# Moving the dilated keys to ScalarE's DMA queue, and the window copies to other places and depths, in a decoder step on one core

## The reference, cut to what matters

```python
# mixing: one projection to q, k, v of two groups of 8 heads
oa_s = stick_breaking(qa_s, k_all, v_all, pos_s, bias_l)     # k_all, v_all: 16 pages a sample
ext_k = jnp.concatenate([cache_dil_k[layer], kb_s], axis=1)  # 2048 old rows and the new one
ext_v = jnp.concatenate([cache_dil_v[layer], vb_s], axis=1)
ob_s = dilated_attention(qb_s, ext_k, ext_v, ...)            # reads 321 of the 2049 rows
dk_s.append(ext_k[:, DEC_SEQ:]); dv_s.append(ext_v[:, DEC_SEQ:])   # outputs: moved by one row
# feed-forward, for each of 256 + 8 rows: 8 heads choose 16 of 16384 experts
u = expert_u[expert]
act = jax.nn.gelu(jnp.einsum('thkd,td->thk', u, h))
return jnp.einsum('thk,thkd->td', (g * act).astype(h.dtype), expert_v[expert])
```

## Time and profile before

| | before |
|---|---|
| median of 3 runs | 1211.17 us (1208.58 to 1219.85) |
| profiled execution, device time | 1215.47 us |
| its span, first to last instruction | 1213.8 us |
| PE, DVE, ACT, POOL busy | 75%, 52%, 29%, 35% of the span |
| bytes moved by DMA | 481.21 MB, mean 396 GB/s |
| share of the DMA engines' time | 76.0% POOL's queue, 22.1% SP's |
| chain that ended last | DMA 46%, PE 30%, issue 8%, DVE 8% |

### The profile page before, as it was taken

One profiled execution on the slowest core, in us unless ns is written; L12 is line 12 of the kernel. 1 busy time (PEld: TensorE's weight loads), 2 busy tenths in 40 slices (PEclk: granted clock), 3 DMA queues, 4 the chain that ended last, 5 costly groups with the idle time before them and its releaser, 6 DMA issues.

```text
span 1213.8 us, 13371 instructions
## 1 busy us (share of the span) xinstructions
PE 909.9 (75%) x3662; PEld 423.6 (35%) x3662; DVE 635.5 (52%) x1604; ACT 351.8 (29%) x959; POOL 420.2 (35%) x430
## 2 busy tenths in 40 slices
PE   2797986668676879964778877877587777777783
PEld 0342443445232448831323322333233322323231
DVE  4200106553222544223776777777777777777755
ACT  0000001463121012221333233323433444244323
POOL 1201323112231000211455554545454455555551
PEclk9799988777898889977999999999999999999996
DMA  9999999988999899999999999999989999999996
GB/s 366 424 379 400 378 365 364 397 338 351 373 392 413 281 367 378 388 396 393 410 414 428 420 428 427 428 428 428 428 357 427 428 427 428 428 428 428 427 427 272
DMA packets 72826, 481.21 MB, mean 396 GB/s; under 512 B 9953, under 2 KB 10306, under 8 KB 27346
## 3 DMA queue, kind: packets, MB, share of 16 engines
q0 software_dynamic: 54720, 377.53, 76.0%
q1 hardware_dynamic: 18066, 103.17, 22.1%
HBM read 477.41 MB, written 70.32 MB: 451 GB/s over the span
## 4 chain that ended last, share of the span: by engine, by line
DMA 46%; PE 30%; issue 8%; DVE 8%; ACT 3%; POOL 2%; SPq 2%; POOLq 0%; DVEq 0%; ACTq 0%
DMA R<-in_uv,idst 29%; PE ps L968 11%; DMA out_dil_v_s<-in_dil_v 6%; DMA R<-in_sb_v,vrow 5%; PE ps L919 5%; PE ps L874 2%; PE ps L576 2%; POOL R L480 2%; DMA R<-in_sb_k 2%; DVE R L1770 2%; DMA vrow<-in_vrow 2%; PE ps L739 2%; PE ps L602 1%; DMA R<-in_uv,idec 1%; ACT wgt L1241 1%
## 5 line engine op out<-in xcount | busy, mean ns | idle before, releaser
L968 PE MATMUL ps<-R,diag 128*128 128x512 f32 x1024 | 491.9, 630 | 168.8 <-ACT diag L1260 167.3
L480 POOL DMA_INDIRECT R<-in_uv,idst x256 | 313.7, 1225 | 365.6 <-PE ps L968 294.6
L1770 DVE CUSTOM_DVE_ANT_0 R<-R,H 128x1024 f32<-128x1024 f32 x264 | 319.3, 1224 | 201.7 <-DMA R<-in_uv,idst 190.7
L968 PEld LDWEIGHTS ps<-R,diag 128*128 128x128 f32 x1024 | 195.7, 199 | 465.0 <-ACT diag L1260 252.0
L1238 ACT ACTIVATE gel<-dots 128x2 f32<-128x2 f32 x132 | 26.8, 203 | 403.9 <-DVE dots L1770 403.9
L576 PE MATMUL ps<-R,HT 128*128 128x512 f32 x192 | 94.3, 631 | 3.9 <-DMA R<-in_wts 3.9
L1260 ACT ACTIVATE diag<-const,wgt 128x128 f32<-128x128 f32 x256 | 88.9, 394 | 14.7 <-PE ps L968 1.4
L310 POOL DMA_INDIRECT R<-in_sb_v,vrow x32 | 30.4, 951 | 114.5 <-PE ps L739 90.2
L432 POOL DMA_DIRECT2D R<-in_wts x24 | 12.8, 541 | 157.3 <-PE ps L874 57.2
L301 POOL DMA_DIRECT2D R<-in_sb_k x64 | 34.7, 542 | 86.5 <-issue 85.9
L1241 ACT ACTIVATE wgt<-gel,gst 128x1 f32<-128x1 f32 x264 | 63.3, 287 | 4.3
(11 more groups left out here) (282 smaller groups left out, 828.6 us busy)
## 6 DMA issues: line engine op xcount, KB each, us to landing
R<-in_wts POOLq DMA_DIRECT2D x48, 1024.0 KB, 17.0
out_dil_k_s<-in_dil_k SPq DMA_DIRECT2D x32, 1023.5 KB
out_dil_v_s<-in_dil_v SPq DMA_DIRECT2D x32, 1023.5 KB
R<-in_sb_k SPq DMA_DIRECT2D x64, 256.0 KB, 8.3
R<-in_sb_k POOLq DMA_DIRECT2D x64, 256.0 KB, 6.7
R<-in_win_v SPq DMA_DIRECT2D x8, 512.0 KB
R<-in_uv,idst POOLq DMA_INDIRECT x256, 11.8
m_all<-in_win_k SPq DMA_DIRECT2D x6, 512.0 KB
```

Of the source, the lines that this page charges most:

```text
L480: pool.indirect_dma_start(out=R[:, row_slot(k), :], out_offset=None, in_=A["uv"], in_offset=bass.IndirectOffsetOnAxis(ap=idst[:, par, k:k ...
L968: last = pe.matmul(ps[:, banks + q, :], diag[:, k % 4, :], R[:, row_slot(k), D + q * 512:D + (q + 1) * 512], start=False, stop=False, skip ...
L1770: dve.tensor_tensor_reduce(u, u, H[:, t, :], 1.0, 0.0, ALU.mult, ALU.add, dots[:, k:k + 1]).then_inc(s["dot_done"], 1)
```

## The change

Four things. (1) The key rows of the dilated heads, `new_rows` of the keys and `window_end` go from SP's program to ACT's, between ACT's other work; `more_keys` is now ACT's. (2) SP then issues the even key pages of samples 1 to 7 in one loop, with nothing between. (3) Ten copies (numbers 26 to 35) are POOL's, issued at once behind the last value pages and ahead of the last eight weight tiles; SP issues the others: 16 early as before, ten where there were four (behind the second sample's window values), and 28 at the end where there were 44. (4) SP keeps six copies under way: each waits for the sixth before it. POOL's ten wait for nothing.

```diff
+COPIES = 8 * NB
+EARLY, POOL_FROM, POOL_COPIES, SP_AHEAD = 16, 26, 10, 6
...
+            def copies(first, end):
+
+                for n in range(first, end):
+                    landed = copied[n % SP_AHEAD]
+                    if n >= SP_AHEAD:
+                        sp.wait_ge(landed, 16 * (n // SP_AHEAD))
+                    copy_piece(sp, n if n < POOL_FROM else n + POOL_COPIES).then_inc(landed, 16)
 
             sp.wait_ge(s["w_used"], 4)
             key_pages(sp, 0, EVEN, first=True)
-            for odd in range(2):
-                copy_windows(0, odd)
-            with sp.Fori(1, 4) as b:
+            copies(0, EARLY)
+            with sp.Fori(1, NB) as b:
                 key_pages(sp, b, EVEN)
...
                 if b == 2:
-                    copy_windows(1, 0, range(2))
+                    copies(EARLY, POOL_FROM)
...
-            copy_windows(1, 0, range(2, 4))
-            for pair, odd in ((1, 1), (2, 0), (2, 1), (3, 0), (3, 1)):
-                copy_windows(pair, odd)
+            copies(POOL_FROM, COPIES - POOL_COPIES)
...
+            for n in range(POOL_FROM, POOL_FROM + POOL_COPIES):
+                copy_piece(pool, n).then_inc(s["copied_pool"], 16)
             weight_rounds(10, CHUNKS // WSLOTS)
...
+            act.wait_ge(s["h_ready"], 3)
+            for b in range(2):
+                window_rows(act, DK, b, b, A["win_k"], dk_ready)
+            act.wait_ge(s["rot_done"], 6)
+            new_rows(act, "dil_k_s", 1, s["new_k"])
+            for b in range(2, 4):
+                window_rows(act, DK, b, b, A["win_k"], dk_ready)
             queries_ev(s["qd_mm"], s["qd_ev"], 5, 1)
+            act.wait_ge(s["new_k"], 32)
+            for b in range(4):
+                window_end(act, DK, b, b, A["dil_k_s"], dk_ready)
             stage_pair(0, QA, KA)
             qkv_ev(2)
+            for b in range(4, 6):
+                more_keys(b)
             turned_pair(0)
             stage_pair(1, QA, KA)
             sticks_logs(0)
+            for b in range(6, NB):
+                more_keys(b)
             turned_pair(1)
```

More of the change, by code:

```diff
@@ L261, in build @@
         dv_ready = [sem(f"dv_ready{n}") for n in range(2)]
-        copied = [sem(f"copied{n}") for n in range(4)]
+        copied = [sem(f"copied{n}") for n in range(SP_AHEAD)]
         e_ready = [sem(f"e_ready{n}") for n in range(NSLOT)]
@@ L313, in value_quad, with copy_piece @@
             ).then_inc(v_ready[m], 16)
+        def copy_piece(eng, n):
+            b, q, m = n // 8, n % 8 // 2, n % 2
+            src, dst = ((A["dil_k"], A["dil_k_s"]), (A["dil_v"], A["dil_v_s"]))[m]
+            size = (PAST - 1) * DG // 4
+            return eng.dma_start(dst[b:b + 1, q * size:(q + 1) * size].rearrange("a (r n) -> (a r) n", r=P),
+                                 src[b:b + 1, q * size + DG:(q + 1) * size + DG].rearrange("a (r n) -> (a r) n", r=P))
         EVEN, ODD = range(0, CPB, 2), range(1, CPB, 2)
@@ L416, in _ @@
             sp.wait_ge(s["new_v"], 32)
-            for n in range(4):
-                sp.wait_ge(copied[n], 16 * 4 * NB // 2)
+            for n in range(SP_AHEAD):
+                sp.wait_ge(copied[n], 16 * len(range(n, COPIES - POOL_COPIES, SP_AHEAD)))
+            sp.wait_ge(s["copied_pool"], 16 * POOL_COPIES)
             sp.wait_ge(s["y_out"], 16 * (2 + QUADS))
@@ L1047, in sticks_exp, with more_keys @@
                 act.activation(aw[2], aw[2], ACT.Exp).then_inc(s["s_e"], 1)
+            def more_keys(b):
+                act.wait_ge(s["dk_used"], b - 3 if b < 6 else b - 1)
+                window_rows(act, DK, b, b % 2, A["win_k"], dk_ready)
+                window_end(act, DK, b, b % 2, A["dil_k_s"], dk_ready)
+            act.wait_ge(s["h_ready"], 3)
[5 more added lines that the diff above has]
+                window_rows(act, DK, b, b, A["win_k"], dk_ready)
             queries_ev(s["qd_mm"], s["qd_ev"], 5, 1)
+            act.wait_ge(s["new_k"], 32)
+            for b in range(4):
+                window_end(act, DK, b, b, A["dil_k_s"], dk_ready)
             stage_pair(0, QA, KA)
             qkv_ev(2)
+            for b in range(4, 6):
+                more_keys(b)
             turned_pair(0)
```

2 lines of the change are left out of this document (1 added, 1 removed).

## The result

| | before | changed |
|---|---|---|
| median, four runs each on one chip | 1210.76 us (1208.58 to 1219.85) | 1239.98 us (1236.77 to 1244.46) |
| ratio to before | | 1.0229 (95% interval 1.0166 to 1.0293) |
| profiled span | 1213.8 us | 1235.1 us |
| eighth, ninth, seventeenth gather issued | 523.65, 531.89, 579.06 | 578.12, 586.68, 601.46 |

The forecast was 1208, within 1188 to 1225.

A forecast was written before the change was run, and what follows sets the result against it. The experts' stage, from about 640 us, was taken as bound by DMA bytes; early copies 0, ACT's keys -1, ten copies +3 gave a shift of +2, and later gathers made the whole -3: 1211.2 - 3 = 1208 us, range 1188 to 1225.

The forecast's parts named there:

- Early copies: Sixteen copies from 50 us, six under way: PE 15 us late, page waits gone, sum 0, between -6 and +15.
- The second credit: Sample 4's pages no longer behind window rows: the 3.46 us wait at 165.35 and 2 us slow clock go, -5.5.
- ACT's keys: Window keys on ACT: DVE starts at 193 instead of 185.88, later waits go; -1 us, between -4 and +7.
- Ten copies: Behind the second sample: 16.5 us of DMA against 12 us slack at 252 to 282; value pages +3 us.
- The shift: Lateness so far when the stage from 390 us begins: 0 - 1 + 3 = +2 us.
- The query projection: Tiles need 22 us beside copies, first landing at 469, second 491; eighth gather out at 557 with the shift.
- the other tiles follow at once: Query projection: once SP's remaining copies end at about 496 us, the later weight tiles come without delay.
- Given back: Gathers after the ninth: idle DMA engines land one every 2.45 us, making up the lateness to -3 us overall.
- how late the ninth gather is: Ninth gather goes out 4 us behind the eighth, at 561 us.
- the end of SP's copies: SP's 18 or 19 remaining copies, beside the query projection's tiles, last to about 496 us.
- a tile at once: POOL's queue passes a whole tile per copy packet, nothing idles: about 1191 us, 1185 to 1198; chance 0.30.
- The slower rival: Early starvation of 15 us not made good, page waits stay with ACT's third queue: 1223, 1218 to 1228; chance 0.22.

The follow-up runs named there:

- e4: Kernel before with only the window keys, new key rows and row ends moved to ACT's queue and SP's even key pages in one loop: 1215.67 us, 1.003.
- e9: Kernel before with six copies under way instead of two, nothing else: 1236.56 us, 1.022.
- e10: Kernel before with ten copies behind the second sample's window values instead of four, nothing else: 1204.30 us, 0.9937.
- e2: Changed kernel with two copies under way for the first sixteen only, six for all later ones: 1236.47 us, 1.0194.
- e3: Changed kernel with no copies on POOL's queue, SP issuing all 64: 1245.23 us, 1.027.
- e15: Kernel before with three large-piece copies under way instead of two: 1232.32 us, 1.0183.
- e5: Changed kernel with six under way for the first 26 copies and two for SP's last 28: 1209.42 us, 1.0001.
- e1: Changed kernel with two of SP's copies under way everywhere instead of six; places, POOL's ten and ACT's keys kept: 1203.55 us, 0.9918.
- e7: Changed kernel with two copies under way everywhere and no copies on POOL's queue: 1205.28 us, 0.9975.
- e11: Changed kernel with two under way, row ends ahead of the queries' copies, and all copies on SP's queue: 1205.86 us, 0.9961.
- e12: Changed kernel with two under way, row ends ahead of the queries' copies, POOL's ten kept: 1204.86 us, 0.9946.
- e13: Kernel before with six copies under way, each in 128 pieces of 8188 bytes instead of 16 of 65504: 1220.13 us, 1.0107.

## Why the prediction was wrong

The forecast had the cause (gapless large packets starve the weight tiles), the places and the early waits right, and the sum wrong: -3 us for what measured +21.3 in the spans.

- **Early copies.** Forecast to end at 95 us at 2.8 us each. The last was issued at 86.41 and its 21 us put its landing at 107: a cycle of 3.5 us. The tile issued at 58.03 was waited for until 90.17 (8.63 us), the next until 104.62 (3.11): 11.7 us of waits and 2.8 of slow clock make the 15 forecast, and with the 7.44 of page wait that went, PE is late by 5.5 (ACT ends the copies of the second third at 137.87 instead of 132.41), as the sum had it. The second credit failed. The wait of 3.46 us at 165.35 did go, but waits of 3.19, 1.49 and 0.95 us at 151 to 168 came in its place, and ACT's last queries' copy is at 196.92, 7.6 late. The early part was +5 to +8 at this point, not 0. That it was the depth that took the wait of 7.44 us away is seen in e4, where it stays (7.4), and in e9, where it goes.
- **ACT's keys.** DVE was to start at 193; it starts at 201.17, 4.2 us behind the row ends' issue at 196.93 (3.3 before, 182.54 to 185.88). Order alone made this 10 us late in e4, and the end 0.3% (3.6 us): within the -4 to +7 given, not the -1 taken.
- **Ten copies.** +3 was forecast at 390 us; e10 measures 9.7. Six copies are 14.7 us of bytes, and the slack gave 6.2 of them (11.9 to 5.7), not 12: the copies' packets run from 250.6 to 291.2 us and pass from the slack into the value pages' full stretch. The six copies fewer behind 390 us more than pay for it, and the part by itself is 0.6% faster.
- **The shift** at the first query tile was +2 by forecast and is 16.6 (452.90 against 436.30): the 7.6 at ACT's last queries' copy and e10's 9.7 make 17.3, against 0 and 3 in the sum.
- **The query projection.** Between first tile issued and eighth gather the forecast adds 31 us, measured are 37.9. Two terms inside were off in opposite directions. A tile does not need 22 us but 16. The prediction read the earlier trace rows as 21 copy packets beside some 25 of 8 KB, "about one for one"; the line's own 43 to 40 packets have the small ones in them, and these take turns too. But "the other tiles follow at once" at 496 us failed: SP's copies last to 537.6. From 406 to 456 us the queues pass 10.60 and 7.27 MB, which are POOL's ten copies, 1 MB of another load of SP's and 5.9 of SP's copies: 3.1 us each and not 2.8, so that 22 were left at 456 instead of 18.5 at 446. They took 3.7 us each instead of 2.7: of the 3.6 us at 472 to 534, the large packet has 2.84 (79.3%) and the weight packets 0.69 (19.3%), against 2.43 and 0.31 in the forecast.
- **Given back.** From the ninth gather to the seventeenth the forecast gives back 32 us (561 against 531.89, to -3), and so does the chip: from 54.8 (586.68 against 531.89) to 22.4 (601.46 against 579.06). This term was right. In e2, e3, e9 and e15, too, about 15 us pass between the ninth and the seventeenth, where before it was 47.

So the step that failed is how late the ninth gather is: +29 by forecast, +54.8 measured. Of the difference, 14.6 are the shift, 6.8 the starving, and 4.6 that the ninth follows the eighth by 8.56 us instead of 4 (it was 8.24 before), less 0.3 of rounding. The term behind it that was most wrong is the end of SP's copies, 496 us by forecast and 537.6 measured.

The prediction had the mechanism of this part: PE's groups stand behind the starved tiles, and once the copies are through the DMA engines idle (20 us in 545 to 587, 0.52 of a share). What it sized wrongly is how late this comes. Some 32 us at the ninth gather can be given back, 54.8 cannot. e5 has a shift of 21.7 us and no starved query projection, and loses nothing (1.0001); e9 has a shift of 4.1 us at the first query tile, is starved, and is as slow. So a shift by copies moved forward is no loss of its own, and starving is one without it. At the eighth gather the two together are much the same (54.5 us in the changed kernel, 51.2 in e9). I read this as one quantity, copies moved forward making the shift and copies left behind the starving; no run shows that by itself. Undoing the early depth (e2) brings 0.35%, within the intervals.

The rivals: a tile at once is out (16 us a tile). The slower rival had the right side, and its sign came too: the values of sample 0 start at 274.66 us on PE, 12.5 later than before. But its mechanism, the early starvation carried through by a third queue, was not the cause of the loss: e2 takes the early starvation away and is still 1.9% slower than before, e4 has the third queue and loses 0.3%, and e9 has no third queue. With 2 and 6 under way compared at both packet sizes the mechanism of the turns stands as shown. On their size, the Trainium skill ("DMA: Bandwidth & Descriptors", "Queues, rings and completion order") says that a whole packet of typically 9 to 17 descriptors is drained before an engine switches; as far as the trace's packets are its descriptors, the runs show one a turn (1141 to 1151 beside 8 KB packets, 576 to 572 and 548 to 550 beside 65504-byte ones, the small ones counted), and the measurement decides.

Two things stay open: whether the 8188-byte pieces are slow for their size or their spacing, and why e1 is 0.8% faster than before while e7, e11 and e12, close to it in build, are 0.25 to 0.54% faster on other chips.

## What to carry to other kernels

Count every packet of a queue, the small ones at the end of a transfer too, when two queues share the DMA engines: here the share of time went by the size of the packets, since the turns were even. A background copy in large packets should leave gaps beside a queue that an engine waits for. Here that meant two transfers under way and not three or six; packets no larger than those of the other queue also ended the starving, but the three runs that had them were 1.1 to 1.4% slower than the kernel before.

Ask of every stage what the waiting engine still has to do when the background traffic ends. If that is long, the DMA engines idle while it is done, and having moved the bytes early gains nothing. Adding up the time lost against the best rate, stretch by stage, before and after, names the stage; the reason has to come from the waits and from runs such as e5 and e9.

## What the runs showed of the hardware

- Two queues that both have work pass one packet each in turn, small packets counted: 1151 to 1141 of about 8 KB (e13, six of SP's transfers under way), and 572 to 576 where SP's large packets are 65504 bytes and POOL's 8 KB.
- A stream of 8 KB packets beside copies in 65504-byte ones gets 1.8 packets for each of them and 19% of the engines' time.
- Copies from memory to memory in separate 8188-byte pieces take 14% longer a byte than in 65504-byte ones with six under way, 9% with two, when nothing else runs.
- With large packets, three copies under way are nearly as bad as six (1.018 and 1.022, two chips); with two, PE waited for no tile of the query projection in the kernel before.
